# A transformer block with 32 experts: the router moved into the output projection, x added last, and the first expert pair written out ahead of the loop

## What is computed

```python
h = rmsnorm(x, norm1_g)
u, q, k, v, g_pool, g_attn = split(h @ w_in)          # 512, 512, 512, 512, 1024, 1024 columns
mix = sigmoid(g_pool) * (pool_mixer(u) @ w_pool_up) + sigmoid(g_attn) * (attention(q, k, v) @ w_attn_up)
x = x + mix @ w_out
h2 = rmsnorm(x, norm2_g)
logits = h2 @ w_router + b_router                     # 32 experts
gate, idx = softmax of the top 4 logits, their experts
for each expert e:                                    # gate_up 1024 x 2048, down 1024 x 1024
    glu, lin = clipped halves of h2[tokens of e] @ w_gate_up[e] + b_gate_up[e]
    y = (glu * sigmoid(1.702 * glu) * (lin + 1)) @ w_down[e] + b_down[e]
    x[tokens of e] += gate * y
```

## Time and profile before

| | us |
|---|---|
| median of 3 runs | 1120.02 |
| the profiled execution, its own time | 1118.15 |
| its span, first to last instruction | 1116.3 |
| TensorE busy | 1013.0 (91%) |
| VectorE, ScalarE, GpSimd busy | 277.6, 187.8, 22.3 |
| mean rate of DMA over the span | 386 GB/s |
| mean granted clock of TensorE | 0.997 |

### The profile page before, as it was taken

How to read it: one execution, slowest core, us unless ns; L and a number is a source line. 1 busy time by engine, 2 the same in 40 slices (tenths; PEclk the granted TensorE clock), 3 DMA queues, 4 the chain that set the end, 5 groups by cost and what they waited for, 6 DMA issues and landing times.

```text
span 1116.3 us, 14173 instructions
## 1 busy us (share of the span) xinstructions
PE 1013.0 (91%) x5749; PEld 484.6 (43%) x5749; DVE 277.6 (25%) x516; ACT 187.8 (17%) x252; POOL 22.3 (2%) x36
## 2 busy tenths in 40 slices
PE   6999997999999988999999888888888988889887
PEld 6989995343434333334333333333333333333333
DVE  5655886211111111111111111111111011111112
ACT  5477433001101010101010101001010100010101
POOL 3200002000000000000000000000000000000000
PEclk9999998999999999999999999999999999999999
DMA  9944479799999999999999999999999999999995
GB/s 317 326 127 128 151 260 400 307 425 427 426 426 426 426 426 423 427 426 427 429 426 426 426 426 427 424 427 427 425 426 427 425 427 425 427 427 427 428 425 216
DMA packets 63041, 431.00 MB, mean 386 GB/s; under 512 B 6364, under 2 KB 27376, under 8 KB 30224
## 3 DMA queue, kind: packets, MB, share of 16 engines
q1 hardware_dynamic: 63016, 430.75, 93.7%
q10 hardware_dynamic: 8, 0.00, 0.0%
HBM read 429.69 MB, written 1.05 MB: 386 GB/s over the span
## 4 chain that ended last, share of the span: by engine, by line
PE 45%; DMA 43%; DVE 6%; issue 2%; SPq 2%; ACT 0%; ACTq 0%; DVEq 0%
PE bank L986 44%; DMA gate_ring<-in_w_gate_up_dram 35%; DMA down_ring<-in_w_down_dram 7%; DVE area_x L967 1%; PE bank L1254 1%; SPq L340 1%; DVE area_m L638 1%; DVE area_x L951 1%; DVE area_x L638 1%; DVE area_x L952 1%; DMA raw<-in_w_in_dram 1%; SPq L390 0%; SPq L398 0%; DVE down_ring L638 0%; DVE w_lo L638 0%
## 5 line engine op out<-in xcount | busy, mean ns | idle before, releaser
L986 PE MATMUL bank<-gate_ring,area_m 128*64 128x512 f32 x2048 | 456.5, 595 | 46.0 <-DMA gate_ring<-in_w_gate_up_dram 44.9
L986 PEld LDWEIGHTS bank<-gate_ring,area_m 128*64 128x64 f32 x2048 | 144.5, 136 | 339.7 <-issue 240.6
L986 PE MATMUL bank<-down_ring,area_x 128*64 128x512 f32 x1024 | 228.8, 596 | 22.7 <-DVE area_x L967 14.3
L951 DVE TENSOR_SCALAR area_x<-bank 128x512 f32<-128x512 f32 x32 | 22.1, 692 | 726.4 <-PE bank L986 726.4
L986 PEld LDWEIGHTS bank<-down_ring,area_x 128*64 128x64 f32 x1024 | 72.1, 137 | 160.7 <-issue 143.2
L986 PE MATMUL bank<-area_m 128*128 128x128 bf16 (+4 forms) x1024 | 121.7, 277 | 1.3 <-ACT area_m L621 1.3
L986 PEld LDWEIGHTS bank<-area_m 128*128 128x128 bf16 (+3 forms) x1024 | 77.3, 114 | 55.9 <-issue 52.1
L613 ACT ACTIVATE area_x<-area_x 128x512 f32<-128x512 f32 x32 | 20.2, 631 | 477.0 <-DVE area_x L951 477.0
L621 ACT ACTIVATE area_m<-bank 64x512 f32<-64x512 f32 x64 | 37.8, 591 | 309.5 <-PE bank L986 309.1
L986 PE MATMUL bank<-w_hi,act_in 128*128 128x256 f32 x320 | 58.5, 284 | 1.6 <-DVE act_in L674 1.6
L986 PE MATMUL bank<-act_in,w_hi 128*128 128x256 f32 x320 | 58.4, 284 | 0.0
(11 more groups left out here) (171 smaller groups left out, 478.1 us busy)
## 6 DMA issues: line engine op xcount, KB each, us to landing
gate_ring<-in_w_gate_up_dram SPq DMA_DIRECT2D x128, 2048.0 KB, 28.3
down_ring<-in_w_down_dram SPq DMA_DIRECT2D x128, 1024.0 KB, 21.8
raw<-in_w_in_dram SPq DMA_DIRECT2D x16, 1024.0 KB, 11.2
raw<-in_w_out_dram SPq DMA_DIRECT2D x4, 1024.0 KB, 5.4
raw<-in_w_pool_up_dram SPq DMA_DIRECT2D x2, 1024.0 KB, 11.5
raw<-in_w_attn_up_dram SPq DMA_DIRECT2D x2, 1024.0 KB, 5.1
area_x<-in_x_dram SPq DMA_DIRECT2D x2, 512.0 KB, 3.8
out_dram<-gate_ring SPq DMA_DIRECT2D x4, 256.0 KB, 2.0
```

The costliest lines, as they stand in the source:

```text
L951: nc.vector.tensor_scalar(glu, glu_b[:], LIMIT, None, ALU.min).then_inc(s_glu, 1)
L986: return nc.tensor.matmul(o, lhsT, rhs, start=start, stop=True, skip_group_check=True)
```

## The change

The second output block is computed tile by tile instead of by column halves, and the eight transposes of x1's first tile stand ahead of its last quarter. Router logits are computed with tokens on the partitions, hT as the stationary operand and router_w moving, one tile after the other, so that there is no transpose behind them. Means, powers, casts, remainders and top 8 go tile by tile; GpSimd's power of the second tile stands behind its constants. The first tile's third part is computed in four pieces by GpSimd, the second's by VectorE. The four `residual` products are gone: x is loaded again after the last use of gate_ring, and VectorE adds it to the finished sums. The gathers of pair 0 follow each other directly, and the steps of the table are called between the chunks of pair 0, which is written out ahead of the loop on TensorE, ScalarE and VectorE; their loops begin at 1. Some pairs of operations over tiles become one. The core of the diff:

```diff
-            sp.wait_ge(s_lgT, 1)
+            sp.wait_ge(s_lg, T)
             load_down(0, 0)
-            sp.wait_ge(s_hn, T)
-            sp.wait_ge(s_p1, T)
+            sp.wait_ge(s_rest, T)
             load_down(0, 2)
-            sp.wait_ge(s_parts, T)
+            sp.wait_ge(s_parts, 4)
+            sp.wait_ge(s_parts_b, 1)
...
+            sp.wait_ge(s_gu, pairs * (2 * KD))
+            for t in range(T):
+                sp.dma_start(x_again[:, 2 * t:2 * t + 2], x_t[:, t].rearrange("p (n f) -> p n f", f=FH)) \
+                  .then_inc(s_again, 16)
...
-                    sp.wait_ge((s_outv, s_outa)[n], t + 1)
-                    sp.dma_start(out_t[t, :, n * FH:(n + 1) * FH], gate_ring[:, 2 * t + n, 0:FH]) \
-                      .then_inc(s_store, 16)
+                    sp.wait_ge(s_outv, 2 * t + n + 1)
+                    sp.dma_start(out_t[t, :, n * FH:(n + 1) * FH], out_sb[:, 2 * t + n]).then_inc(s_store, 16)
...
-            power(tiny[:, 4:6], tiny[:, 2:4], T).then_inc(s_rstd, 1)
+            power(tiny[:, 4:5], tiny[:, 2:3], 1).then_inc(s_rstd, 1)
             pool.wait_ge(s_rstd, 4)
             pool.wait_ge(s_wo, 2 * T)
...
-            for t in range(T):
-                pool.wait_ge(s_p1, T + t + 1)
-                nc.gpsimd.tensor_tensor(parts[:, t, 2 * D:3 * D], rest[:, t], parts[:, t, D:2 * D], ALU.subtract) \
-                    .then_inc(s_parts, 1)
-                pool.wait_ge(s_parts, t + 1)
+            pool.wait_ge(s_mean, 5)
+            power(tiny[:, 5:6], tiny[:, 3:4], 1).then_inc(s_rstd, 1)
+            pool.wait_ge(s_rstd, 5)
+            pool.wait_ge(s_p1, T + 1)
+            QW = D // 4
+            for q in range(4):
+                nc.gpsimd.tensor_tensor(parts[:, 0, 2 * D + q * QW:2 * D + (q + 1) * QW],
+                                        rest[:, 0, q * QW:(q + 1) * QW],
+                                        parts[:, 0, D + q * QW:D + (q + 1) * QW], ALU.subtract).then_inc(s_parts, 1)
+            pool.wait_ge(s_parts, 4)
...
-            for t in range(T):
+                act.wait_ge(s_hnT, t + 1)
+                for k in range(KD // 2, KD):
+                    nc.scalar.activation(hT[:, k, t * P:(t + 1) * P], bank[5 + 2 * t][:, (k % 4) * P:(k % 4 + 1) * P],
+                                         ACT.Copy, scale=cols[:, ROW_G2 + k:ROW_G2 + k + 1]).then_inc(s_hT3, 1)
+                act.wait_ge(s_rstd, 4 + t)
                 nc.scalar.activation(parts[:, t, 0:D], x1[:, t], ACT.Copy, scale=tiny[:, 4 + t:5 + t]) \
                     .then_inc(s_p1, 1)
...
+            def pair(i):
...
+            act.wait_ge(s_tab, 1)
+            nc.scalar.activation(o_T, t_b[0:E, :].rearrange("p (a n) -> p a n", n=P), ACT.Copy).then_inc(s_oTT, 1)
+            pair(0)
+            act.wait_ge(s_table, 1)
+            pairs = act.value_load(item_table[0:1, COLS:COLS + 1], min_val=E // 2, max_val=ITEMS // 2)
+            with act.Fori(1, pairs) as i:
+                pair(i)
...
-                for t in range(T):
-                    dve.wait_ge(s_wo, 2 * n + t + 1)
-                    last = tt(x1[:, t, n * FH:(n + 1) * FH], acc[2 * t + n][:], x_sb[:, t, n * FH:(n + 1) * FH],
-                              ALU.add)
-                    if n == 1:
-                        last.then_inc(s_x1, 1)
-            dve.wait_ge(s_sumsq, 7)
...
+            def add_x(n, t):
+                dve.wait_ge(s_wo, 2 * n + t + 1)
+                return tt(x1[:, t, n * FH:(n + 1) * FH], acc[2 * t + n][:], x_sb[:, t, n * FH:(n + 1) * FH], ALU.add)
+            def mean_square(t):
+                dve.wait_ge(s_sumsq, 6 + t)
+                mean(3 + t, (tiny[:, 2 + t:3 + t], tiny[:, t:t + 1]), D)
...
+            def router_in(t):
...
+            def remainder(t):
                 dve.wait_ge(s_p1, t + 1)
-                tt(rest[:, t], rest[:, t], parts[:, t, 0:D], ALU.subtract).then_inc(s_rest, 1)
-            dve.wait_ge(s_lg, 1)
-            link(nc.vector.tensor_reduce(r_lg, bank[5][:, 0:T * P].rearrange("p (t c e) -> p t e c", c=COLT, e=E),
...
+            def top(t):
+                dve.wait_ge(s_lg, t + 1)
+                dve.wait_ge(s_rstd, 4 + t)
+                link(nc.vector.scalar_tensor_tensor(out=r_lg[:, t], in0=bank[4 + 2 * t][:, 0:E],
+                                                    scalar=tiny[:, 4 + t:5 + t], in1=router_b[:], op0=ALU.mult,
+                                                    op1=ALU.add))
...
-            tt(r_p, r_top, r_top[:, :, 0:1].to_broadcast([P, T, 8]), ALU.subtract).then_inc(s_soft, 1)
-            link(nc.vector.tensor_copy(r_idf, r_idx))
+                link(nc.vector.max_index(r_idx[:, t], r_top[:, t], r_lg[:, t]))
+            add_x(0, 0)
+            add_x(0, 1)
+            add_x(1, 0).then_inc(s_x1, 1)
+            mean_square(0)
+            router_in(0)
+            add_x(1, 1).then_inc(s_x1, 1)
+            remainder(0)
+            mean_square(1)
+            router_in(1)
+            top(0)
...
+            top(0)
+            remainder(1)
+            top(1)
...
+            link(tt(eq4, r_iota.unsqueeze(1).unsqueeze(1).to_broadcast([P, T, TOP_K, E]),
+                    r_idx[:, :, 0:TOP_K].unsqueeze(3).to_broadcast([P, T, TOP_K, E]), ALU.is_equal))
...
+            nc.vector.memset(tiny[:, 63:64], 0.0).then_inc(s_sr, 1)
+            dve.wait_ge(s_p1, 2 * T)
+            tt(parts[:, 1, 2 * D:3 * D], rest[:, 1], parts[:, 1, D:2 * D], ALU.subtract).then_inc(s_parts_b, 1)
+            selector(0, slice(0, 1), s_sela)
+            dve.wait_ge(s_gps, 1)
+            dve.wait_ge(s_g2, 16)
+            evacuate_gather(0)
             dve.wait_ge(s_softe, 1)
...
+            dve.wait_ge(s_gps, 2)
+            evacuate_gather(1)
             link(tt(r_p, r_p, r_s[:, 0:T].unsqueeze(2).to_broadcast([P, T, 8]), ALU.mult))
...
+            dve.wait_ge(s_tab, 2)
+            cnt = y_b[0:E, 0:MAX_OVER]
...
+            last.then_inc(s_tabv, 1)
+            dve.wait_ge(s_tab, 4)
...
+            pair(0, lambda at, n: slice(at, at + n))
+            dve.wait_ge(s_table, 1)
+            pairs = dve.value_load(item_table[0:1, COLS:COLS + 1], min_val=E // 2, max_val=ITEMS // 2)
+            with dve.Fori(1, pairs) as i:
+                pair(i, bass.ds)
...
+                dve.wait_ge(s_again, 16 * T)
+                for n in range(2):
+                    dve.wait_ge(s_sum, 2 * t + n + 1)
+                    tt(out_sb[:, 2 * t + n], acc[2 * t + n][:], x_again[:, 2 * t + n], ALU.add).then_inc(s_outv, 1)
...
+            def x1_transposed(t):
                 pe.wait_ge(s_x1, t + 1)
                 for k in range(KD):
-                    last = nc.tensor.transpose(bank[4 + k // 2][:, (k % 2) * S + t * P:(k % 2) * S + (t + 1) * P],
+                    last = nc.tensor.transpose(bank[4 + 2 * t + k // 4][:, (k % 4) * P:(k % 4 + 1) * P],
                                                x1[:, t, k * P:(k + 1) * P], ident[:])
-            last.then_inc(s_hnT, 1)
-            for k in range(KD):
...
+            def router(t, ks):
+                for k in ks:
+                    if k == 0:
+                        pe.wait_ge(s_hT2, t + 1)
+                    if k >= KD // 2:
+                        pe.wait_ge(s_hT3, t * (KD // 2) + k - KD // 2 + 1)
+                    last = mm(bank[4 + 2 * t][:, 0:E], hT[:, k, t * P:(t + 1) * P], router_w[:, k, :], k == 0)
+                if k == KD - 1:
+                    last.then_inc(s_lg, 1)
+            project(BLOCKS.index("out0"), [acc[0], acc[2]], merged_there, s_wo)
+            b = BLOCKS.index("out1")
...
+                for h in range(2):
+                    if t == 0:
+                        wait_split(b, h)
+                    for k in range(KD):
+                        last = mm3(acc[1 + 2 * t][:, h * HB:(h + 1) * HB], acts(k, t * P, P), weights(b, h, k * HB, HB),
+                                   h == 0 and k == 0)
+                    if t == 1 and h == 0:
+                        last.then_inc(s_first, 1)
+                        x1_transposed(0)
+                last.then_inc(s_wo, 1)
+            router(0, range(0, KD // 2))
+            x1_transposed(1)
+            router(0, range(KD // 2, KD))
+            router(1, range(KD))
...
+            pe.wait_ge(s_const, N_CONST)
+            mm(lin_b[:, 0:E], below_bf[:], r_sel[:, 0], True)
+            mm(lin_b[:, E:2 * E], ones_bf[:], r_sel[:, 0], False)
...
+            def gather(r, third=None):
                 o = (t_b, y_b)[r]
-                for k in range(4 * r, 4 * r + 4):
-                    for t in range(T):
-                        for part in range(3):
+                first = True
+                for t in range(T):
+                    for part in range(3):
+                        if third and part == 2:
+                            third(t)
+                        for k in range(4 * r, 4 * r + 4):
                             lo = part * D + k // 2 * 2 * P
```

(68 more changed lines are left out.)

177 lines of the change are left out of this document (44 added, 133 removed).

## The result

| | before | after |
|---|---|---|
| median | 1120.59 us (4 runs, 1118.64 to 1122.06) | 1112.92 us (4 runs, 1111.6 to 1114.91) |
| ratio | | 0.9939, interval 0.9923 to 0.9955 |
| profiled execution, span | 1118.15, 1116.3 us | 1111.6, 1109.8 us |

A forecast was written before the change was run, and what follows sets the result against it. The stream of expert weights at 426 GB/s bounds the loop, so only its holes and tail can be won. 8.0 - 1.0 - 0.1 = 6.9 us takes the median from 1120.02 to 1113.1 us, range 1110.8 to 1117.0.

The forecast's parts named there:

- the hole before pair 0: Weight stream at 195 to 210 us, between the prefill's end and the loop's first load: 8.0 us unused, would close.
- the one at 175: Hole in the weight stream at 175 to 180 us, 1.6 us unused: would grow by 1.0 us as out1 ends later.
- its bounds: Top-8 selection before the ranks: ready at 185.4 against 187.88 before, at earliest 184.2 and at latest 186.8.
- Held, they cost 1 us each: Two router logit updates on VectorE beside GpSimd's subtractions: 1 us each if held, 0.2 if free; free was taken.
- The lead of a load: First loop load before pair 0's hole: data 0.7 us after issue, so needed by 196.8, expected 196.3, slack 0.5 us.
- The gathers: 48 gather matmuls before pair 0: 5.2 us, at half clock because the clock rises some 5 us after dense work begins.
- margin of 0.6 us: First down loads in pair 0: issued at 216.6 while the queue lasts until 217.2, against a margin of 3.0 before.
- The tail: End of the kernel: second load of x hidden, last output step a VectorE add for a ScalarE copy, +0.1 us.
- Late issue: Rival: first loop load comes late, hole before pair 0 stays open by 0.9 to 4.4 us, 1114 to 1117.5; chance 0.25.
- late down loads: Rival: waits for table steps in pair 0 open a new hole at 217 us, 1 to 2 us, 1114.6; chance 0.08.
- a router that doesn't shorten: Rival: GpSimd's second power waits behind its constants, selection stays at 187.9, gain 4.9 us, 1115.1; chance 0.08.
- Code fetch: Rival: instruction fetch for written-out pair 0 waits behind queued loads, TensorE stands 12.7 us, 5.3 us slower, 1125.3; chance 0.05.

The follow-up runs named there:

- early down load: Pair 0's last down chunk loaded before two gate loads that wait for out1's end: 1.0002 in the kernel before, 0.9947 in the changed kernel.
- once TensorE came sooner: Changed kernel with the early down load and residual products put back in TensorE's idle time: ratio 0.9924 to the kernel before.
- delays of TensorE: Changed kernel with two or eight unused products before pair 0, or the table steps ahead of it: ratios 0.9948, 0.9998, 1.0029 to the kernel before.
- extra products: Changed kernel with eight, or two, unused 512-column products between the gathers and pair 0: ratio 0.9998, or 0.9948, to the kernel before.
- transposes behind: Changed kernel with the first tile's eight transposes behind out1's end, as in the kernel before: ratio 0.9962 to the kernel before.

## Why the prediction was right

- **The bound and the sum.** Right, the mechanism included. The stream of weights sets the loop, the hole before pair 0 was worth 8.0 us and closed (430 GB/s), the one at 175 grew by 0.9 where 1.0 was forecast, and the prefill landed at about 197.2, for 197.5. The two early down loads show the mechanism best: the same megabyte moved ahead gave nothing in either kernel alone, and 1.2 us once TensorE came sooner.
- **The selection came too early for its bounds.** Forecast 185.4, bounds 184.2 to 186.8; it was ready at 183.4. Two steps were wrong. GpSimd's 3.2 us of constants were taken over unchanged, and took 2.2, because, as far as the ends of the rows show, the operation of VectorE that had held them (L825) was folded into another. And the comparison was taken to wait for GpSimd's last piece, which ended at 183.94; it waited only for the piece under way, to 182.50. "Held, they cost 1 us each" misread the two updates of the earlier trace rows, of which one was held for 1.91 us and the other not at all. That the new updates read PSUM and so run free was right, 0.24 us. Pair 0's biases came at 190.05, not 192.0. The Trainium skill (GPSIMD Engine Reference, Specifications) names contention with VectorE instructions that have two SBUF inputs. The trace agrees for GpSimd's subtractions (1.91 and 0.71 us), not for its memset beside L831 (0.19 us).
- **The lead of a load was too small by 1 to 2 us.** "Data followed the issue by 0.7 us" took the first half-full window for the full stream; in the same trace 1.7 us of the stream are lost behind the issue. By the delays of TensorE (slack 0.3, 0.5 and 1.3 us) the lead is 1.6 to 2.6. With it, the first issue was needed by 194.6 to 195.6, not 196.8, and the forecast's own 196.3 would have left a hole of 0.7 to 1.7 us. The 2.0 us gained in the selection paid for it. That the slack came out at 0.5 us is luck, the difference of two wrong dates, and so is a part of the hit on the time.
- **The gathers.** 5.2 us forecast, 5.25 measured, at half clock to 189.9, some 5 us after they began, as the step said.
- **In pair 0.** The down loads were issued at 214.50, against 216.6, and no hole followed. The margin of 0.6 us was counted without a lead as well: issued at 216.6, with the queue lasting to 217.2, they would have been late by the same lead.
- **The tail.** +0.5 us in place of +0.1: from the last gate chunks (1085.32 and 1092.36) to the end it took 24.5 us against 23.9. The add has its 0.1; the rest is the last store, whose issue ended at 1107.13 and which landed 2.7 us later, against 2.3 before. It was 2.5 to 2.7 in every kernel that loads x again, and 2.3 in the others. Why is open.
- **The rivals.** Late issue, late down loads and a router that doesn't shorten: none occurred as written, though the extra products, the early down load and the transposes behind show the first two a microsecond or less away. Code fetch: the instruction queue moved 15 packets in place of 13, and no idle of TensorE without a cause stands ahead of pair 0.

## What to carry to other kernels

Where a stream of loads bounds a kernel, list its holes and ask of each which side ends it: the consumer that frees a buffer, or the loads that come late. When both sides are within a microsecond, moving one gives nothing, and an idle engine's time is the place for work (here the residual) that brings its clock back or keeps it up. A chain that is moved or folded changes its neighbours' contention too, so take durations of its pieces one by one, with what ran beside them: a mean over two, one held and one free, fits neither.

## What the runs showed of the hardware

- A load had to be issued some 1.6 to 2.6 us before the queue ran dry to leave no hole (an estimate from three delays, 2.2, 7.0 and 11.9 us, that cost 1.8, 6.5 and 10.6), though its first data came within about 1 us: after its issue at 202.77 the kernel before lost 1.7 us of the full stream.
- GpSimd and VectorE took turns by whole instructions where GpSimd subtracted and VectorE had two SBUF inputs: a 32-column update ended with a subtraction of 2.13 us and so took 1.91, beside pieces of 0.66 us a comparison took 0.71 in place of 0.42, and the piece behind it 0.85.
- GpSimd's iota and memset took 0.53 and 0.71 us beside VectorE's product of a 1024-wide SBUF tensor with a scalar, and 0.13 and 0.19 in the changed kernel, the memset beside an operation with two SBUF inputs.
- Removing 3.8 us of TensorE work made nothing faster in the kernel before: the clock came back 0.8 us later against out1's end, and fell to 0.50 again for the first 2.9 us of pair 0, which took 15.35 us in place of 13.91 for eight chunks.
- Router products with 128-column stationary and 32-column moving operands took 3.01 us for 24 records, 0.125 each, as the transposes' row had suggested.
